# Branch D's value products in pairs of heads, with features on partitions

## The chip, the cores and the metric

The kernel runs on one core of a Trainium2 chip, in one launch. The metric is the device time of that core in microseconds (us), from the start to the end of the program. Three runs of the kernel before gave 691.07, 691.10 and 691.25 us, so the median is 691.1 us.

## What is computed

The model has two layers (DEPTH 2) over 512 positions of width 1024. In each layer the input is normalised and multiplied by one wide matrix `w_in`. Its columns feed four attention branches of four heads each: A (latent), B (dilated), C (sparse, top 128 keys of each query) and D (differential). Each branch's output is multiplied by SiLU of a gate, the four are put side by side and multiplied by `w_out`. Branch D is the one that changes:

```python
def diff_branch(q, k, v, lam_params, subln, table, lambda_init):
    ...
    p = jax.nn.softmax(s, axis=-1)
    a = p[:, 0] - lam * p[:, 1]
    return jnp.einsum('bhqs,bshd->bqhd', a.astype(v.dtype), v)
    ...
    o = rms_norm(o, subln) * (1.0 - lambda_init)
```

Each head has two softmax maps. They are combined with a learned weight, multiplied by the values (64 features a head), and every row of 64 features is normalised by its own root mean square and scaled by `subln`.

## The kernel before

There are no loops that the hardware runs: the Python writes out one long instruction stream for each engine. The order is the text `SCHEDULE` (line 109 on), a list of steps by hand. `sequence()` turns it into one list of (layer, step), and each engine's block walks the same list from the first step to the last and emits what that step wants of it. So an engine that stands at a wait of one step starts nothing of the later steps, and where a step stands in the text decides what lies ahead of it in each queue.

The steps that matter here:

- `unit X c`: 24 matmuls of TensorE (three products for each of 8 slices of the contraction) that give 128 columns of the projection for 512 tokens. ScalarE writes the rounded high part out of PSUM (line 815), VectorE writes the rest (line 1044). Units take turns in two PSUM banks.
- `CONVERT_AT` (from `convert_steps`): after some steps ScalarE turns the next weights into their high part (line 726, two instructions), and GpSimd makes the low part (line 684). The function puts a conversion where steps of a certain cost have passed since the buffer came free: a token unit costs 1, another unit 2, a `pv` 1.
- `scores j a b`: products of queries and keys of job j, blocks a to b-1, through three PSUM banks in turn. VectorE adds the bias (line 1085, "shifted"), which frees the bank, then ScalarE takes the exponential (line 834). Jobs 0 to 3 are branch D's heads, with 8 blocks each (two maps of 4), jobs 4 to 7 are B's.
- `norm j`: for D, VectorE combines the two maps (lines 989 to 994).
- `turn j kb`: TensorE transposes a block column of probabilities into one of two PSUM banks (line 1365), and ScalarE copies it to `turned[j % 2]` (line 847), which frees the bank. TensorE's `turn` waits until the copy of the turn two before it is done. The first copy of job j waits for the `pv` of job j - 2.
- `pv i`: the product with the values. TensorE waits until every `turn` of its jobs is copied. For D one head is one step with 10 small matmuls, queries on partitions (line 1386). For B, C and A a pair of heads is one step with 8 matmuls, features on partitions, the two heads in the two halves of the partitions (line 1393).
- For D, VectorE multiplies each head by the reciprocal of its sum into `od` (line 1104). `dsquares` squares and sums on VectorE (1116 to 1118), GpSimd takes the power -1/2 (line 691), `dscale` multiplies (1123), `dnorm` transposes on TensorE (1402) and multiplies into the gate (1130).
- For B, C and A, `wide i` spreads the reciprocals over 512 columns on ScalarE (line 857), `spread i` transposes them on TensorE (1411) and VectorE multiplies them into the gate (1095); VectorE then multiplies the product in (1111).
- `topk n`: n rounds of the selection for branch C, all on VectorE (lines 980 and 981).

Of the kernel before, what the change touches and what calls it, by code (L numbers as in the profile page):

```python
# [39 lines left out]
for _n, _w in (("cq", 192), ("ckv", 128), ("kr", 32), ("ga", 256), ("bq", 256), ("bk", 256), ("bv", 256),  # L40
# [45 lines left out]
NWIDE = NPV - HEADS  # L86
# [31 lines left out]
    scores 7 0 3, topk 1, topk 2, turn 5 2, fill 8, norm 6, turn 5 3, topk 1, unit gc 0, fill 9, topk 3, scores 7 3 4, unit gc 1, norm 7, turn 6 0, fill 10, spread 4, fill 11, pv 4, turn 6 1, turn 6 2  # L118
    scores 8 0 2, turn 6 3, turn 7 0, scores 8 2 4, wide 5, turn 7 1, unit ga 0, aload, turn 7 2, turn 7 3, spread 5, pv 5
    scores 9 0 1, turn 8 0, turn 8 1, norm 8, aup_head, unit ga 1, mix 6, turn 8 2, scores 9 1 4, aup 0, turn 8 3, aup 1, turn 9 0, norm 9  # L120
    scores 10 0 1, turn 9 1, aturn 0, wide 6, scores 10 1 4, aup 2
    scores 11 0 1, turn 9 2, scores 11 1 4, norm 10, spread 6, turn 9 3, aturn 1, pv 6, aup 3, turn 10 0, aturn 2, turn 10 1, turn 10 2, mix 7, norm 11, turn 10 3, aturn 3, turn 11 0, turn 11 1, wide 7
    scores 12 0 2, scores 12 2 4
    scores 13 0 2, spread 7, turn 11 2, turn 11 3, scores 13 2 4, norm 12, mix 3, pv 7, mix 2, turn 12 0, turn 12 1, turn 12 2, norm 13, turn 12 3, turn 13 0
    scores 14 0 2, turn 13 1, wide 8, turn 13 2, scores 14 2 4
    scores 15 0 1, norm 14, mix 4, mix 5, turn 13 3, scores 15 1 4, spread 8, norm 15, turn 14 0, pv 8, ya 0, wide 9, turn 14 1, turn 14 2, turn 14 3, turn 15 0, turn 15 1, spread 9, turn 15 2, turn 15 3, ya 2, pv 9, mix 0, mix 1, ya 1
# [39 lines left out]
def units_of(step):  # L166

    k = step[0]
    if k == "u":
        return ["dve", "dve"]  # L170
    if k == "unit":
        if step[1] in ("cv", "dv", "bv", "ckv"):
            return ["act"]
        return ["act"] if step[1:] == ("cq", 0) else ["dve"]
    if k in ("dnorm", "spread"):
# [44 lines left out]
ROOTS = [(l, s) for l, s in SEQUENCE if s[0] in ("hmean", "dsquares", "aup_head", "y")]  # L220
# [67 lines left out]
def trunk(nc, x, w_in, w_out, norm_pre, norm_post, mla_q_norm, mla_kv_norm, mla_w_uq, mla_w_ukv,  # L288
# [8 lines left out]
    with ExitStack() as ctx:  # L297
# [60 lines left out]
        odsq = at("odsq", "staging", [P, NB, 2, HD], F32)  # L358
# [3 lines left out]
        od = at("od", "staging", [P, NB, 2, HD], F32, skip=2 * KB)  # L362
# [40 lines left out]
        dsum = tiny("dsum", [P, 2 * NB])  # L403
# [53 lines left out]
        od_ready, a_folded, lat_squared = sem("od_ready"), sem("a_folded"), sem("lat_squared")  # L457
# [29 lines left out]
        def gate_of(i):  # L487

            br, h = JOBS[PV_JOBS[i][0]]
            return 2 * "ABC".index(br) + h // 2  # L490

        def wait_gated(eng, l, k):

            if k >= 6:
                eng.wait_ge(emptied_by["dve"], emptied(l * NU + UNIT_AT[("dnorm", k - 6)], "dve"))
# [220 lines left out]
        def _(act):  # L716
# [44 lines left out]
            for l, step in SEQUENCE:  # L761
# [15 lines left out]
                if kind == "unit":  # L777
# [8 lines left out]
                    if name in ("bv",):  # L786
                        act.wait_ge(pv_ready, l * NPV + HEADS)
# [48 lines left out]
                if kind == "turn":  # L836
# [5 lines left out]
                    if kb == 0 and j == 0 and l > 0:  # L842
# [5 lines left out]
                                         ACT.Copy).then_inc(turn_emptied, 1)  # L848
                if kind == "wide":
# [65 lines left out]
        def _(dve):  # L915
# [42 lines left out]

            after(nc.vector.memset(means[:], 1.0))
# [23 lines left out]
            def normalise(l, j):  # L983
# [3 lines left out]
                if MAPS[j] == 2:  # L987
# [3 lines left out]
                                                         ALU.mult, ALU.mult))  # L991
                    for q in range(NB):
# [8 lines left out]
            for l, step in SEQUENCE:  # L1001
# [88 lines left out]
                if kind == "spread":  # L1090
                    n = l * NU + UNIT_AT[step]
                    k = gate_of(step[1])
                    wait_unit_emptied(dve, l * NU + UNIT_AT[("unit", "g" + "abcd"[k // 2], k % 2)])
                    dve.wait_ge(unit_ready, n + 1)
                    nc.vector.tensor_tensor(gate[:, k, :], bank[:, unit_bank(n), :], gate[:, k, :], ALU.mult  # L1095
                                            ).then_inc(emptied_by["dve"], 1)
                if kind == "pv":
                    j = PV_JOBS[step[1]][0]
                    br, h = JOBS[j]
                    dve.wait_ge(pv_ready, l * NPV + step[1] + 1)  # L1100
                    if br == "D":
                        if h % 2 == 0 and (h > 0 or l > 0):
                            dve.wait_ge(unit_ready, (l if h else l - 1) * NU + UNIT_AT[("dnorm", 0 if h else 1)] + 1)
                        nc.vector.tensor_tensor(od[:, :, h % 2, :],
                                                bank[:, PV, 0:NB * HD].rearrange("p (t d) -> p t d", d=HD),
                                                inv[:, j % 4, 0, :].unsqueeze(2).to_broadcast([P, NB, HD]),
                                                ALU.mult).then_inc(pv_emptied, 1)
                    else:
                        k = gate_of(step[1])
# [3 lines left out]
                if kind == "dsquares":  # L1113
                    r = ROOT_AT[l, step]
                    dve.wait_ge(pv_emptied, l * NPV + 2 * step[1] + 2)
                    after(nc.vector.tensor_tensor(odsq[:], od[:], od[:], ALU.mult))
                    after(nc.vector.tensor_reduce(dsum[:].rearrange("p (t h) -> p t h", h=2), odsq[:], AX_X, ALU.add))
                    nc.vector.tensor_scalar(means[:, r % 2, :], dsum[:], 1.0 / HD, EPS, ALU.mult, ALU.add
                                            ).then_inc(means_ready, 1)
                if kind == "dscale":  # L1120
                    r = ROOT_AT[l, ("dsquares", step[1])]
                    dve.wait_ge(roots_ready, r + 1)
                    nc.vector.tensor_tensor(od[:], od[:],
                                            roots[:, r, :].rearrange("p (t h) -> p t h", h=2).unsqueeze(3)
                                            .to_broadcast([P, NB, 2, HD]), ALU.mult).then_inc(od_ready, 1)
                if kind == "dnorm":
                    n = l * NU + UNIT_AT[step]
                    k = 6 + step[1]
# [49 lines left out]
                if kind == "y":  # L1178
# [4 lines left out]
                    after(nc.vector.tensor_tensor(dsum[:, 0:1], ysq[:, tb, 0:1], ysq[:, tb, 1:2], ALU.add))  # L1183
                    nc.vector.tensor_scalar(means[:, r % 2, 0:1], dsum[:, 0:1], 1.0 / DM, EPS,
# [16 lines left out]
        def _(pe):  # L1201
# [61 lines left out]
            for l, step in SEQUENCE:  # L1263
# [104 lines left out]
                if kind == "pv":  # L1368
# [11 lines left out]
                    if br == "D":  # L1380
# [143 lines left out]
```

## Time and profile before

| | |
|---|---|
| median of 3 runs | 691.1 us |
| span of the profiled execution | 689.9 us |
| TensorE matmul busy | 665.3 us, 96% |
| VectorE busy | 394.1 us, 57% |
| ScalarE busy | 338.7 us, 49% |
| GpSimd busy | 241.9 us, 35% |

The span runs from the first to the last instruction; the 1.2 us between it and the median lie outside of it. The granted clock of TensorE is 0.999 of full speed on average. The two layers repeat each other: what layer 0 does at a time t in the stretch of branch D, layer 1 does at t + 333.8 us.

### The profile page before, as it was taken

How to read it: one execution, taken by the hardware profiler on the slowest of the kernel's cores; microseconds unless marked ns; L12 is line 12 of the kernel's file. 1: busy time of each engine (PE TensorE's matmuls, PEld its weight loads, DVE VectorE, ACT ScalarE, POOL GpSimd, SP SyncE). 2: the span in 40 equal slices, each digit the busy share in tenths (PEclk: the TensorE clock that was granted, in tenths of full speed). 3: DMA queues.
4: the chain of work that ended last, by engine and by line, in shares of the span. 5: the costliest groups of instructions: out<-in, count | busy, mean ns of one | idle time of the engine just before them, and what ended most of it. 6: DMA issues, size and time to landing. Idle time of an engine off the chain costs nothing. (4 is left out here: it accounts for less than half of the span.)

```text
span 689.9 us, 10538 instructions
## 1 busy us (share of the span) xinstructions
PE 665.3 (96%) x3852; PEld 538.4 (78%) x3852; DVE 394.1 (57%) x982; ACT 338.7 (49%) x804; POOL 241.9 (35%) x209
## 2 busy tenths in 40 slices
PE   6999999999999999999999999999999999999996
PEld 4988877788887665679998897878788777556995
DVE  4413599868669375540470257985968755555114
ACT  5523634666333647952353355456543553787120
POOL 1442541434242942002424534325422467020030
PEclk9999999999999999999999999999999999999999
DMA  8448877323222213012362697552322220120202
GB/s 252 138 169 223 240 216 254 124 78 109 76 77 77 78 61 123 1 43 82 124 183 76 214 273 207 146 152 77 110 77 76 77 78 23 58 104 1 92 31 92
DMA packets 68763, 80.97 MB, mean 117 GB/s; under 512 B 12853, under 2 KB 54453, under 8 KB 68713
## 3 DMA queue, kind: packets, MB, share of 16 engines
q1 hardware_dynamic: 68713, 80.31, 38.1%
q8 instruction: 31, 0.51, 0.3%
q14 instruction: 19, 0.16, 0.1%
HBM read 69.77 MB, written 13.94 MB: 121 GB/s over the span
## 5 line engine op out<-in xcount | busy, mean ns | idle before, releaser
L684 POOL TENSOR_TENSOR w_low<-w_raw,w_high 128x512 fp32r<-128x512 f32 (+2 forms) x156 | 199.8, 1313 | 364.2 <-ACT w_high L726 364.1
L1236 PE MATMUL bank<-uT,w_high 128*128 128x512 f32 x400 | 159.7, 399 | 0.0
L1238 PE MATMUL bank<-uT,w_low 128*128 128x512 f32 x400 | 157.8, 394 | 0.0
L1237 PE MATMUL bank<-uT,w_high 128*128 128x512 f32 x400 | 157.4, 393 | 0.0
L834 ACT ACTIVATE probs<-probs,negmax 128x128 f32<-128x128 f32 (+3 forms) x160 | 88.8, 557 | 51.6 <-DVE negmax L1085 50.4
L726 ACT ACTIVATE w_high<-w_raw 128x1024 fp32r<-128x1024 f32 (+2 forms) x78 | 76.4, 1031 | 28.5 <-DMA w_raw<-in_w_out 24.4
L1236 PEld LDWEIGHTS bank<-uT,w_high 128*128 128x128 f32 x400 | 75.2, 188 | 17.4 <-issue 1.4
L1238 PEld LDWEIGHTS bank<-uT,w_low 128*128 128x128 f32 x400 | 75.0, 188 | 17.7
L1237 PEld LDWEIGHTS bank<-uT,w_high 128*128 128x128 f32 x400 | 75.2, 188 | 16.2
L1236 PE MATMUL bank<-w_high,mix 128*128 128x256 f32 x256 | 72.1, 282 | 0.2 <-DVE gate L1095 0.2
L1237 PE MATMUL bank<-w_low,mix 128*128 128x256 f32 x256 | 71.6, 280 | 0.0
L1238 PE MATMUL bank<-w_high,mix 128*128 128x256 f32 x256 | 71.6, 280 | 0.0
L1236 PE MATMUL bank<-w_high,uT 128*128 128x256 f32 (+1 forms) x192 | 56.5, 294 | 1.1 <-DVE uT L955 0.7
L1365 PE MATMUL bank<-ident,probs 128*128 128x128 f32 x320 | 52.1, 280 | 4.6 <-ACT turned L847 3.5
L1237 PE MATMUL bank<-w_low,uT 128*128 128x256 f32 (+1 forms) x192 | 55.1, 287 | 0.0
L1238 PE MATMUL bank<-w_high,uT 128*128 128x256 f32 (+1 forms) x192 | 55.0, 287 | 0.0
L980 DVE MAX8 best<-select 128x8 f32<-128x512 f32 (+2 forms) x96 | 53.6, 558 | 2.1
L847 ACT ACTIVATE turned<-bank 128x512 f32<-128x512 f32 (+3 forms) x128 | 50.6, 428 | 6.9 <-PE bank L1365 4.4
L1365 PEld LDWEIGHTS bank<-ident,probs 128*128 128x128 f32 x320 | 37.1, 140 | 19.8 <-ACT turned L847 7.7
L1085 DVE CUSTOM_DVE_ANT_0 probs<-bank,strips 128x128 f32<-128x128 f32 (+1 forms) x104 | 45.0, 471 | 13.0 <-PE bank L1238 10.5
L981 DVE MATCH_REPLACE8 select<-best,select 128x512 f32<-128x512 f32 (+2 forms) x96 | 52.1, 543 | 0.0
L1236 PEld LDWEIGHTS bank<-w_high,mix 128*128 128x128 f32 x256 | 48.2, 188 | 0.9 <-issue 0.5
(153 smaller groups left out, 1048.1 us busy)
## 6 DMA issues: line engine op xcount, KB each, us to landing
w_raw<-in_w_in SPq DMA_DIRECT2D x27, 1024.0 KB, 5.5
w_raw<-in_w_out SPq DMA_DIRECT2D x8, 1024.0 KB, 4.9
parts_dram<-staging SPq DMA_DIRECT2D x12, 512.0 KB, 5.6
strips<-strips_dram SPq DMA_DIRECT2D x24, 256.0 KB, 5.6
dqk<-parts_dram SPq DMA_DIRECT2D x24, 256.0 KB, 4.4
hX<-in_x SPq DMA_DIRECT2D x8, 512.0 KB, 5.4
qidx<-parts_dram SPq DMA_DIRECT2D x12, 256.0 KB, 4.3
w_raw<-in_w_in SPq DMA_DIRECT2D x4, 512.0 KB, 5.6
```

Of the source, the lines that this page charges most:

```text
L684: ins = nc.gpsimd.tensor_tensor(w_low[:, s, ks, 0:w], w_raw[:, s, ks, 0:w], w_high[:, s, ks, 0:w].bitcast(F32), ALU.subtract)
L726: nc.scalar.activation(w_high[:, g % SLOTS, ks, 0:w], w_raw[:, g % SLOTS, ks, 0:w], ACT.Copy).then_inc(w_high_done, 1)
L834: nc.scalar.activation(pr, pr, ACT.Exp, bias=negmax[:, j % 4, m, q:q + 1], scale=-1.0, accum_out=sums[:, j % 4, m, q:q + 1]).then_inc(exp_ ...
L847: nc.scalar.activation(turned[j % 2][:, TOFF[kb]:TOFF[kb] + w], bank[:, TURN + t % 2, 0:w], ACT.Copy).then_inc(turn_emptied, 1)
L980: after(nc.vector.max(best[:], row))
L981: after(nc.vector.match_replace(row, best[:], row, MARK))
L1085: nc.vector.tensor_tensor_reduce(sl, bank[:, SCORE + n % 3, 0:WID[q]], bias, -1.0, 3.0e38, ALU.add, ALU.min, negmax[:, j % 4, m, q:q + 1]) ...
L1236: nc.tensor.matmul(out_ap, lh, rh, start=start, stop=False)
L1237: nc.tensor.matmul(out_ap, lh, rl, start=False, stop=False)
L1238: return nc.tensor.matmul(out_ap, ll, rh, start=False, stop=stop)
L1365: ins = nc.tensor.transpose(bank[:, TURN + t % 2, (q - kb) * P:(q - kb + 1) * P], buf[:, POFF[q] + kb * P:POFF[q] + (kb + 1) * P], ident[:])
```

## The change

Branch D's products go as the other branches' do: `PV_JOBS` holds pairs for all heads, so `pv 0` takes jobs 0 and 1, `pv 1` jobs 2 and 3, and the old `pv 4` to `pv 9` become `pv 2` to `pv 7`. The steps `dsquares`, `dscale` and `dnorm` go. In their place ScalarE squares the product out of PSUM into `dsq`, and the new step `dsum` multiplies `dsq` by a 128x2 matrix of ones and zeros (`pairs`), which gives the sums of squares of the two heads for each query. VectorE makes means of them, with an epsilon multiplied by the squared sum of the exponentials, so that the division by that sum drops out. GpSimd takes the roots as before, and `wide` and `spread` bring them into rows.

```diff
-PV_JOBS = [(j,) for j in range(HEADS)] + [(j, j + 1) for j in range(HEADS, NJ, 2)]
+PV_JOBS = [(j, j + 1) for j in range(0, NJ, 2)]
...
-    scores 2 0 2, norm 1, unit bq 0, scores 2 2 3, topk 1, unit bq 1, turn 1 0, turn 1 1, scores 2 3 6, pv 0, scores 2 6 8, norm 2, turn 1 2, turn 1 3, unit bk 0, turn 2 0, turn 2 1
-    scores 3 0 1, scores 3 1 4, turn 2 2, topk 4, unit bk 1, scores 3 4 6, pv 1, scores 3 6 8, turn 2 3, dsquares 0, norm 3, dscale 0, squares_a
-    scores 4 0 3, unit cqq 0, turn 3 0, dnorm 0, scores 4 3 4, topk 5, turn 3 1, pv 2, unit cqq 1, turn 3 2
-    scores 5 0 2, turn 3 3, topk 1, unit ck 0, turn 4 0, norm 4, turn 4 1, topk 1, scores 5 2 4, topk 1, turn 4 2, turn 4 3, topk 1, pv 3, topk 1, topk 1, topk 1, unit ck 1, topk 1
-    scores 6 0 1, unit bv 0, topk 1, unit bv 1, unit bv 2, norm 5, dsquares 1, scores 6 1 4, dscale 1, topk 1, turn 5 0, turn 5 1, asums, topk 1, topk 2, unit bv 3, topk 1, topk 1, topk 1, wide 4, dnorm 1
...
+    scores 2 0 2, norm 1, unit bq 0, scores 2 2 3, topk 1, unit bq 1, turn 1 0, turn 1 1, scores 2 3 6, turn 1 2, turn 1 3, scores 2 6 8, norm 2, pv 0, unit bk 0, turn 2 0, turn 2 1, dsum 0
+    scores 3 0 1, scores 3 1 4, turn 2 2, topk 4, unit bk 1, scores 3 4 6, scores 3 6 8, turn 2 3, wide 0, norm 3, squares_a
+    scores 4 0 3, unit cqq 0, turn 3 0, spread 0, scores 4 3 4, topk 5, turn 3 1, unit cqq 1, turn 3 2
+    scores 5 0 2, turn 3 3, topk 1, pv 1, unit ck 0, turn 4 0, norm 4, turn 4 1, topk 1, scores 5 2 4, topk 1, dsum 1, turn 4 2, turn 4 3, topk 1, topk 1, topk 1, wide 1, topk 1, unit ck 1, topk 1
+    scores 6 0 1, unit bv 0, topk 1, unit bv 1, unit bv 2, norm 5, spread 1, scores 6 1 4, topk 1, turn 5 0, turn 5 1, asums, topk 1, topk 2, unit bv 3, topk 1, topk 1, topk 1, wide 2
...
@@ scalar @@
+                if kind == "pv" and step[1] < NPD:
+                    i = step[1]
...
+                    act.wait_ge(pv_ready, l * NPV + i + 1)
+                    nc.scalar.activation(dsq[:], bank[:, PV, :], ACT.Square).then_inc(d_squared, 1)
...
+                    if i < NPD:
+                        r = ROOT_AT[l, ("dsum", i)]
+                        act.wait_ge(roots_ready, r + 1)
+                        nc.scalar.activation(wide[i % 2][:].rearrange("p q h d -> p (q h) d"),
+                                             roots[:, r, :].unsqueeze(2).to_broadcast([P, 2 * NB, HD]),
+                                             ACT.Copy).then_inc(wide_ready, 1)
@@ vector @@
+                    nc.vector.scalar_tensor_tensor(desq[:, j, :], sums[:, i, 0], EPS, sums[:, i, 0],
+                                                   ALU.mult, ALU.mult)
...
+                        dve.wait_ge(d_squared, l * NPD + step[1] + 1)
+                        nc.vector.scalar_tensor_tensor(gate[:, k, :], bank[:, PV, :], subln[:, l:l + 1],
+                                                       gate[:, k, :], ALU.mult, ALU.mult).then_inc(pv_emptied, 1)
...
+                if kind == "dsum":
...
+                    nc.vector.scalar_tensor_tensor(means[:, r % 2, :].rearrange("p (t h) -> p t h", h=2),
+                                                   bank[:, unit_bank(n), 0:2 * NB].rearrange("p (t h) -> p t h", h=2),
+                                                   1.0 / HD, desq[:, 2 * i:2 * i + 2, :].rearrange("p h t -> p t h"),
+                                                   ALU.mult, ALU.add).then_inc(means_ready, 1)
+                    nc.vector.tensor_copy(ysum[:], bank[:, unit_bank(n), 0:1]).then_inc(emptied_by["dve"], 1)
@@ tensor @@
-                    if br == "D":
-                        hs = slice(HD * h, HD * (h + 1))
-                        tr = turned[j % 2]
-                        for q in range(NB):
-                            for kb in range(q + 1):
-                                a = TOFF[kb] + (q - kb) * P
-                                ins = nc.tensor.matmul(bank[:, PV, HD * q:HD * (q + 1)], tr[:, a:a + P], v[:, kb, hs],
-                                                       start=kb == 0, stop=kb == q)
...
+                if kind == "dsum":
...
+                    pe.wait_ge(d_squared, l * NPD + step[1] + 1)
+                    b = work_bank(n)
+                    for q in range(NB):
+                        ins = nc.tensor.matmul(b[:, 2 * q:2 * q + 2], dsq[:, q * P:(q + 1) * P], pairs[:],
+                                               start=True, stop=True)
```

`pv` steps count in `convert_steps`. With the new schedule the weights `bv` (group 13) are converted at `unit cqq 1` and no longer at the old `pv 2`; the other conversions keep their places.

## Rows read from the trace of the kernel before

**Rows 1.** The page's busy times, by engine, with instructions.

```profile
PE 665.3 (96%) x3852; PEld 538.4 (78%) x3852; DVE 394.1 (57%) x982; ACT 338.7 (49%) x804; POOL 241.9 (35%) x209
```

**Rows 2.** Busy times by stretch: us, engines, clock, DMA share, GB/s; D's stretch of layer 0.

```profile
139.00:215.00 76.00, 75.49 (x445) 62.73 (x444) 57.14 (x165) 38.78 (x97) 27.04 (x21) 1.00 0.28 89
```

**Rows 3.** Timeline of TensorE around pv 0: start, length, line, idle before.

```profile
139.51 2.34 PE L1386 MATMUL bank<-values,turned 128*128 128x64 f32 x20
141.66 0.65 PE L1339 MATMUL bank<-dqk 96*128 96x384 f32 x2
142.15 0.49 PE L1365 MATMUL bank<-ident,probs 128*128 128x128 f32 x3
142.40 0.48 PE L1236 MATMUL bank<-uT,w_high 128*128 128x512 f32 x1
```

**Rows 4.** Timeline of TensorE, a pair of branch B and what follows it.

```profile
226.49 2.37 PE L1393 MATMUL bank<-turned,values 128*64 128x512 f32 x16
228.80 0.55 PE L1365 MATMUL bank<-ident,probs 128*128 128x128 f32 x3
229.56 0.44 PE L1365 MATMUL bank<-ident,probs 128*128 128x128 f32 x2 [0.22 <-ACT turned L847]
```

**Rows 5.** Timeline of ScalarE around pv 0.

```profile
139.03 2.00 ACT L726 ACTIVATE w_high<-w_raw 128x1024 fp32r<-128x1024 f32 x2
140.92 0.97 ACT L847 ACTIVATE turned<-bank 128x512 f32<-128x512 f32 x2
...
143.35 0.61 ACT L834 ACTIVATE probs<-probs,negmax 128x384 f32<-128x384 f32 x1
...
144.66 0.54 ACT L847 ACTIVATE turned<-bank 128x256 f32<-128x256 f32 x2
```

**Rows 6.** Timeline of TensorE around the old pv 1.

```profile
156.24 2.34 PE L1386 MATMUL bank<-values,turned 128*128 128x64 f32 x20
...
160.94 0.50 PE L1236 MATMUL bank<-uT,w_high 128*128 128x512 f32 x1
```

**Rows 7.** Timeline of VectorE around the old pv 1.

```profile
156.98 0.69 DVE L1044 SCALAR_TENSOR_TENSOR bqk<-bank,bqk 128x512 fp32r<-128x512 f32 x1 [0.82 <-ACT bqk L815]
157.58 0.28 DVE L1085 CUSTOM_DVE_ANT_0 probs<-bank,strips 128x128 f32<-128x128 f32 x1
...
159.47 0.69 DVE L1085 CUSTOM_DVE_ANT_0 probs<-bank,strips 128x512 f32<-128x512 f32 x1
```

**Rows 8.** Timeline of ScalarE around unit cqq 1 and turn 3 3.

```profile
176.92 0.60 ACT L815 ACTIVATE cqk<-bank 128x512 fp32r<-128x512 f32 x1 [3.52 <-PE bank L1238]
177.42 0.38 ACT L847 ACTIVATE turned<-bank 128x256 f32<-128x256 f32 x1
178.48 0.40 ACT L834 ACTIVATE probs<-probs,negmax 128x128 f32<-128x128 f32 x1 [0.69 <-DVE negmax L1085]
...
179.38 0.25 ACT L847 ACTIVATE turned<-bank 128x128 f32<-128x128 f32 x1
```

**Rows 9.** Timeline of TensorE there: turns 3 2 and 3 3, unit ck 0.

```profile
176.66 0.38 PE L1365 MATMUL bank<-ident,probs 128*128 128x128 f32 x2
...
177.86 0.33 PE L1365 MATMUL bank<-ident,probs 128*128 128x128 f32 x1
177.94 0.48 PE L1236 MATMUL bank<-uT,w_high 128*128 128x512 f32 x1
```

**Rows 10.** Timeline of VectorE at norm 0: the small instruction.

```profile
115.33 0.22 DVE L990 SCALAR_TENSOR_TENSOR coef<-inv,neglam,sums 128x4 f32<-128x4 f32 x1
```

**Rows 11.** Timeline of ScalarE in layer 1: its copies of turns 1 0 and 1 1.

```profile
474.70 0.97 ACT L847 ACTIVATE turned<-bank 128x512 f32<-128x512 f32 x2
```

**Rows 12.** Timeline of TensorE: the last matmul.

```profile
682.87 0.28 PE L1238 MATMUL bank<-w_high,mix 128*128 128x256 f32 x1
```

**Rows 13.** Busy times by stretch after the last matmul, columns as in rows 2.

```profile
685.00:687.00 2.00, 0.00 (x0) 0.00 (x0) 1.75 (x2) 0.00 (x0) 0.00 (x0) 1.00 0.00 0
687.00:689.00 2.00, 0.00 (x0) 0.00 (x0) 0.00 (x0) 0.00 (x0) 0.00 (x0) 0.81 0.64 262
```

More of the change, by code:

```diff
@@ new lines @@
+    scores 5 0 2, turn 3 3, topk 1, pv 1, unit ck 0, turn 4 0, norm 4, turn 4 1, topk 1, scores 5 2 4, topk 1, dsum 1, turn 4 2, turn 4 3, topk 1, topk 1, topk 1, wide 1, topk 1, unit ck 1, topk 1
+    scores 6 0 1, unit bv 0, topk 1, unit bv 1, unit bv 2, norm 5, spread 1, scores 6 1 4, topk 1, turn 5 0, turn 5 1, asums, topk 1, topk 2, unit bv 3, topk 1, topk 1, topk 1, wide 2
+    scores 7 0 3, topk 1, topk 2, turn 5 2, fill 8, norm 6, turn 5 3, topk 1, unit gc 0, fill 9, topk 3, scores 7 3 4, unit gc 1, norm 7, turn 6 0, fill 10, spread 2, fill 11, pv 2, turn 6 1, turn 6 2
@@ L120 @@
+    scores 8 0 2, turn 6 3, turn 7 0, scores 8 2 4, wide 3, turn 7 1, unit ga 0, aload, turn 7 2, turn 7 3, spread 3, pv 3
     scores 9 0 1, turn 8 0, turn 8 1, norm 8, aup_head, unit ga 1, mix 6, turn 8 2, scores 9 1 4, aup 0, turn 8 3, aup 1, turn 9 0, norm 9
-    scores 10 0 1, turn 9 1, aturn 0, wide 6, scores 10 1 4, aup 2
-    scores 11 0 1, turn 9 2, scores 11 1 4, norm 10, spread 6, turn 9 3, aturn 1, pv 6, aup 3, turn 10 0, aturn 2, turn 10 1, turn 10 2, mix 7, norm 11, turn 10 3, aturn 3, turn 11 0, turn 11 1, wide 7
+    scores 10 0 1, turn 9 1, aturn 0, wide 4, scores 10 1 4, aup 2
@@ L127 @@
+    scores 14 0 2, turn 13 1, wide 6, turn 13 2, scores 14 2 4
+    scores 15 0 1, norm 14, mix 4, mix 5, turn 13 3, scores 15 1 4, spread 6, norm 15, turn 14 0, pv 6, ya 0, wide 7, turn 14 1, turn 14 2, turn 14 3, turn 15 0, turn 15 1, spread 7, turn 15 2, turn 15 3, ya 2, pv 7, mix 0, mix 1, ya 1
 """
@@ L174, in units_of @@
         return ["act"] if step[1:] == ("cq", 0) else ["dve"]
-    if k in ("dnorm", "spread"):
+    if k in ("dsum", "spread"):
         return ["dve"]
@@ L216, in highs @@
     return full * UNIT_HIGH.count(True) + UNIT_HIGH[:rest].count(True)
-ROOTS = [(l, s) for l, s in SEQUENCE if s[0] in ("hmean", "dsquares", "aup_head", "y")]
+ROOTS = [(l, s) for l, s in SEQUENCE if s[0] in ("hmean", "dsum", "aup_head", "y")]
 ROOT_AT = {r: i for i, r in enumerate(ROOTS)}
@@ L402, in trunk @@
         ysq = tiny("ysq", [P, NB, 2])
-        dsum = tiny("dsum", [P, 2 * NB])
+        desq = tiny("desq", [P, HEADS, NB])
+        ysum = tiny("ysum", [P, 1])
+        pairs = tiny("pairs", [P, 2])
         means = tiny("means", [P, 2, 8])
@@ L489, in gate_of @@
             br, h = JOBS[PV_JOBS[i][0]]
[L490 removed]
+            return 2 * "ABCD".index(br) + h // 2
         def wait_gated(eng, l, k):
             if k >= 6:
[L495 removed]
+                wait_unit_emptied(eng, l * NU + UNIT_AT[("spread", k - 6)])
             else:
@@ L956, in low_u @@
                                             uT[:, 0, ks, ts].bitcast(F32), ALU.subtract).then_inc(emptied_by["dve"], 1)
+            for half in range(2):
+                for h in range(2):
+                    nc.vector.memset(pairs[HD * half:HD * (half + 1), h:h + 1], float(h == half))
             after(nc.vector.memset(means[:], 1.0))
@@ L1097, in _ @@
                 if kind == "pv":
-                    j = PV_JOBS[step[1]][0]
-                    br, h = JOBS[j]
-                    dve.wait_ge(pv_ready, l * NPV + step[1] + 1)
-                    if br == "D":
[L1102 to L1107, printed above, removed]
+                    k = gate_of(step[1])
+                    if step[1] < NPD:
+                        wait_unit_emptied(dve, l * NU + UNIT_AT[("unit", "gd", k % 2)])
+                        dve.wait_ge(d_squared, l * NPD + step[1] + 1)
+                        nc.vector.scalar_tensor_tensor(gate[:, k, :], bank[:, PV, :], subln[:, l:l + 1],
+                                                       gate[:, k, :], ALU.mult, ALU.mult).then_inc(pv_emptied, 1)
                     else:
-                        k = gate_of(step[1])
+                        dve.wait_ge(pv_ready, l * NPV + step[1] + 1)
                         wait_unit_emptied(dve, l * NU + UNIT_AT[("spread", step[1])])
@@ L1112, in _ @@
                                                        ALU.mult, ALU.mult).then_inc(pv_emptied, 1)
-                if kind == "dsquares":
+                if kind == "dsum":
+                    i = step[1]
+                    n = l * NU + UNIT_AT[step]
                     r = ROOT_AT[l, step]
[L1115 to L1128, printed above, removed]
-                    dve.wait_ge(unit_ready, n + 1)
-                    nc.vector.scalar_tensor_tensor(gate[:, k, :], bank[:, unit_bank(n), :], subln[:, l:l + 1],
-                                                   gate[:, k, :], ALU.mult, ALU.mult).then_inc(emptied_by["dve"], 1)
+                    dve.wait_ge(unit_ready, n + 1)
+                    nc.vector.scalar_tensor_tensor(means[:, r % 2, :].rearrange("p (t h) -> p t h", h=2),
[3 more added lines that the diff above has]
+                    nc.vector.tensor_copy(ysum[:], bank[:, unit_bank(n), 0:1]).then_inc(emptied_by["dve"], 1)
                 if kind == "aup_head":
@@ L1182, in _ @@
                     dve.wait_ge(roots_ready, r - 1)
-                    after(nc.vector.tensor_tensor(dsum[:, 0:1], ysq[:, tb, 0:1], ysq[:, tb, 1:2], ALU.add))
-                    nc.vector.tensor_scalar(means[:, r % 2, 0:1], dsum[:, 0:1], 1.0 / DM, EPS,
+                    after(nc.vector.tensor_tensor(ysum[:], ysq[:, tb, 0:1], ysq[:, tb, 1:2], ALU.add))
+                    nc.vector.tensor_scalar(means[:, r % 2, 0:1], ysum[:], 1.0 / DM, EPS,
                                             ALU.mult, ALU.add).then_inc(means_ready, 1)
```

59 lines of the change are left out of this document (27 added, 32 removed).

## The prediction

> **What bounds the kernel.** I read the busy times first. TensorE's matmuls fill 96% of the span and no other engine passes 57% [rows 1]. In the stretch of branch D they fill 75.5 of 76 us at full clock [rows 2]. So a matmul that goes saves its time, and a wait of TensorE that comes costs its time. VectorE and ScalarE count only where they hold TensorE up. That is read from the timelines, step by step in the order of the schedule: what each engine has in its queue ahead of what TensorE waits for. Layer 1 repeats layer 0: its copies of turns 1 0 and 1 1 begin at 474.70, those of layer 0 at 140.92 [rows 5, 11]. I walk through layer 0 and double the result.
>
> **The matmuls.** A single head of D holds TensorE from 139.51 to 141.66, 2.15 us for 20 passes of 128x64, or 0.107 each [rows 3]. A pair of another branch takes 226.49 to 228.80, 2.31 us for two heads [rows 4]. Per layer four singles (8.60) become two pairs (4.62), 3.98 less. Each `dsum` adds 4 matmuls with a stationary 128x128 block, in the same two passes as D's singles, so 8. No row shows two moving columns. I take the 0.107 of the passes of 64 columns, whose stationary block has the same size, so 0.86 a step and 1.72 a layer. The low end is half a pass price, 0.43; the high end is 8 passes that don't overlap at all, 2.2 (the 0.275 of one record's length). `spread 0` and `spread 1` are four transposes each in the place of the four of `dnorm`: nothing. Work alone is -2.26 us a layer.
>
> The page TensorEngine Tiling (Array Packing) of the Trainium skill, section Performance Considerations, speaks for the swap: with a moving side of 64 or less, swap the operands and tile the columns twice. The rows agree (2.31 for two heads against 4.30), so by that rule alone the change gains.
>
> **VectorE, ScalarE, GpSimd.** VectorE loses some 4 us a pair and gains about 2. ScalarE gains one square and one `wide`. None of this is on the path as busy time: VectorE is idle before most of these places. The roots have time: `dsum 0` is over before unit bk 1 (5.7 us), its root is wanted after it; `dsum 1` is followed by unit ck 1. One small thing is on the path: the instruction for `desq` stands ahead of the four that combine the maps of job 0, and `turn 0 0` waits for those. It costs as much as L990 at most, 0.22 [rows 10]; I take 0.15 a layer, with 0 to 0.25 as ends.
>
> **The waits, in the order of the schedule.** Here lies the price. `pv 0` and `pv 1` stood where TensorE would otherwise have waited; now they go elsewhere.
>
> Place 1, turns 1 2 and 1 3. TensorE has written turns 1 0 and 1 1 before 139.5, but ScalarE is converting weights until 141.0 and copies them from 140.92 to 141.89 [rows 5]. `turn 1 2` needs the first of the two banks. Before, `pv 0` lay between and nothing was lost: turns 1 2 and 1 3 went at 142.15 [rows 3]. Now `turn 1 2` is due at 139.51 and waits until about 141.55, `turn 1 3` until 141.95. Two score blocks follow to about 142.6 (they took 0.49 [rows 3]).
>
> Place 2, the pair `pv 0` waits for the copy of `turn 1 3`. ScalarE's queue has turns 1 0 and 1 1, three exponentials until 143.35 [rows 5], and then the two copies, which took 0.54 [rows 5]: 143.9. With 0.05 for the restart the pair runs from 143.95 to 146.26 and unit bk 0 starts at 146.26 where it started at 142.40 [rows 3]. Places 1 and 2: +3.86, of which 3.7 is waiting (2.0 and 1.35, and restarts). Behind the waiting TensorE stands everything.
>
> `dsum 0`: +0.86.
>
> Place 3, the score blocks of job 3 without the old `pv 1` between them. Block 7 needs the bank of block 4, which VectorE shifts from 157.58 to 157.86, behind the low part of unit bk 1 [rows 7]. TensorE would be ready at 156.5. With VectorE's four shifts close up, the last starts at 158.6 and not at 159.47 [rows 7], and all behind it (the blocks of job 4, then unit cqq 0 at 160.94 [rows 6]) moves by that: -0.87 where a single [rows 6] of 2.15 us went. So 1.28 becomes a wait.
>
> The old `pv 2` goes: -2.15. It stood ahead of cqq 1 with nothing waiting, so this one is a true gain.
>
> Place 4, the pair `pv 1` right behind `turn 3 3`. Call T the end of unit cqq 1 (176.66 [rows 9]). Before, ScalarE wrote cqq 1's high part to T+0.76, copied turn 3 2, waited for the shifts, took two exponentials and copied turn 3 3 at T+2.72 to T+2.97 [rows 8]; nobody hurried, since unit ck 0 started at T+1.28 [rows 9]. Now the pair needs that copy. And the conversion of `bv` (2.0 us, as in rows 5) falls to cqq 1 and lies in front: high part to T+0.76, conversion to T+2.7, turn 3 2 to T+3.0, exponentials (0.90 [rows 8]) to T+3.9, copy to T+4.13. The pair starts at T+4.18, ends at T+6.49, and ck 0 starts 5.21 later than before, 2.9 of it waiting.
>
> `dsum 1` +0.86, the old `pv 3` -2.15. Behind it nothing waits: VectorE's rounds of `topk` decide the low part of ck 1, some 1.5 us behind TensorE, and the next use of that bank comes over 3 us after it.
>
> **The sum.** Per layer 3.86 + 0.86 - 0.87 - 2.15 + 5.21 + 0.86 - 2.15 + 0.15 = +5.8 us; that is -2.1 of work and +7.9 of waits. Twice is +11.5. The profiled execution had a span of 689.9, so 701.4, and the median lies 1.2 above the span: 702.6. Downstream I find nothing to take it back: in the rest of a layer TensorE waits only briefly, and for copies that move with it.
>
> **Rivals.** *Work alone decides*, if ScalarE's queue is not as full as I read it: 2 x (-2.1) = -4.2, 686.9, faster. For it: TensorE is the bound. Against it: the copies at 140.92 are in the trace behind the conversion, and a turn of TensorE is seen to wait for such a copy even behind a pair (0.22 [rows 4]). A chance of 0.11, since two of the four waits would have to go before the sign turns (from 5.8 saved a layer on).
>
> *The conversion at cqq 1 does not stand in the way* (it moves, or I have its place wrong). Then `pv 1` starts at T+3.0 at the latest row, some 1.1 earlier, with shifts that come sooner up to 1.9: -2.3 to -3.8, 698.8 to 700.3. A chance of 0.12.
>
> *The clock falls in the new waits.* Price: matmuls at 1.2 in place of 2.4 GHz take double; if that lasted as long as one unit of 5.7 us in each layer, +5.7 each, 714. Against it: the last matmul ends at 683.15 [rows 12] and the granted clock is still 1.00 until 687, falling only then [rows 13]; that is 3.8 us idle, and my longest wait is 2.9. A chance of 0.04. The page TensorE: Matmul & The Clock Gate of the Trainium skill, Part 1, says that an idle TensorE is throttled to half rate and that gaps in the middle of a kernel cost this way; the trace agrees for its tail only.
>
> *A part of the waits is absorbed later* so that the time ends within 0.2% (1.4 us, about what a measurement of this kernel can tell from no change): 0.03. The forecast itself has 0.70.
>
> **The range.** The unknown of `dsum` gives -1.7 to +5.4 in all, `desq` -0.3 to +0.2, and restarts after four waits a layer, at 0.05 to 0.2 each, up to +1.2. They don't add up at their ends. With the second rival that is 698 to 707. Slower by over 0.2%: 0.86, within: 0.03, faster: 0.11.
>
> **What would show it.** In the profile after, TensorE's turn line (L1365's successor) should wait about 2 us for the copy in front of turn 1 2, once a layer; the line of the pairs should wait 1.3 and 2.9 us for copies in front of `pv 0` and `pv 1`; ScalarE should run the conversion right behind the high part of cqq 1; the eight passes of `dsum` should take 0.9 us; TensorE's busy time should fall by about 4 us while the span grows. I am wrong if the pairs of D start without a wait, if `dsum` takes over 2 us a step, or if the granted clock drops inside the span.

## The result and the profile after

The changed kernel takes 712.5 us (median of four runs, 706.3 to 719.6) against 691.1 before. The ratio is 1.029, with a 95% interval of 1.024 to 1.034. It is slower, as forecast, but by 21 us and not by 11.5, outside of the range. Its runs differ by 13 us among themselves, those of the kernel before by 2, and the slower a run the lower its mean granted clock of TensorE: 0.988 at 706.3, 0.983 at 711.7, 0.979 at 713.4 and 0.969 at 719.6, the run that was profiled. The kernel before has 0.995 to 0.999 in the runs beside the experiments. The run of 719.6 us counts as a slow one and is left out of the ratio; the other three have a median of 711.7.

The lines below are of that slowest run, so they show the loss at its largest; the profile of experiment e3, at 713.7 us, has low stretches of the clock at the same three places of each layer, three of the six half as long.

The page of the kernel after, first the busy times (to set beside rows 1), then TensorE's granted clock in 40 slices, in tenths:

```profile
PE 678.7 (95%) x3788; PEld 536.8 (75%) x3788; DVE 385.5 (54%) x982; ACT 343.0 (48%) x812; POOL 239.8 (33%) x209
...
PEclk9999999988899999999999999998889999999999
```

There are 64 matmul records fewer and yet TensorE is busy for 13 us more. The clock row (PEclk, 9 stands for 90% or more) says why: in three slices of each layer it ran below full speed. Those are the slices of branch D.

Who TensorE waited for in branch D's stretch of layer 0 (columns: us in total, times, longest). In the kernel before there was one wait here, of 0.5 us; the lines of before, L1365, L1393 and L1339, are L1376, L1395 and L1350 now:

```profile
PE bank L1395 <- ACT turned L848: 3.4, 2, 2.6
PE bank L1376 <- ACT turned L848: 1.9, 1, 1.9
PE bank L1350 <- DVE negmax L1105: 1.5, 2, 1.3
```

TensorE's timeline around turns 1 2 and 1 3 and the pair `pv 0`, which answers to rows 3 and, for the form of the pair, to rows 4 (start, length, what, idle before):

```profile
138.33 0.71 PE L1350 MATMUL bank<-dqk 96*128 96x512 f32 x3
140.94 0.83 PE L1376 MATMUL bank<-ident,probs 128*128 128x128 f32 x3 [1.90 <-ACT turned L848]
141.42 1.09 PE L1350 MATMUL bank<-dqk 96*128 96x384 f32 x2
143.32 4.54 PE L1395 MATMUL bank<-turned,values 128*64 128x512 f32 x16 [0.81 <-ACT turned L848]
147.78 0.69 PE L1247 MATMUL bank<-uT,w_high 128*128 128x512 f32 x1
```

Both waits are where the prediction put them; the second is 0.81 us and not 1.35, since the score blocks ahead of it took longer. But the pair takes from 143.32 to 147.78, 4.46 us, where the same form took 2.31 in rows 4. ScalarE in the same stretch, to set beside rows 5:

```profile
138.40 1.99 ACT L727 ACTIVATE w_high<-w_raw 128x1024 fp32r<-128x1024 f32 x2
140.29 0.97 ACT L848 ACTIVATE turned<-bank 128x512 f32<-128x512 f32 x2
...
142.72 0.54 ACT L848 ACTIVATE turned<-bank 128x256 f32<-128x256 f32 x2
```

Busy times by stretch (columns as in rows 2; the number before the last two is the granted clock), first from turns 1 2 on, then around place 3, then around place 4:

```profile
139.00:141.00 2.00, 0.10 (x2) 0.07 (x2) 1.47 (x7) 2.00 (x4) 1.48 (x2) 1.00 0.97 261
141.00:148.00 7.00, 6.19 (x22) 2.65 (x23) 3.62 (x11) 3.66 (x14) 3.49 (x3) 0.53 0.34 111
148.00:150.00 2.00, 2.00 (x9) 1.64 (x10) 0.75 (x1) 0.50 (x1) 0.00 (x0) 0.95 0.00 0
...
165.00:172.00 7.00, 7.00 (x20) 5.42 (x20) 5.25 (x15) 5.16 (x17) 4.08 (x4) 0.52 0.64 215
...
186.00:193.00 7.00, 6.19 (x21) 3.18 (x22) 0.99 (x2) 1.35 (x6) 3.52 (x3) 0.53 0.36 125
```

A clock of 0.52 in a stretch of 7 us is 1.2 GHz in nearly all of it, the lower of the two levels. The first two begin when TensorE is at work again, at 141.4 and 165.3 us, 2.3 and 2.5 us after it had stopped. The third begins at 185.8, 1.5 us after it had stopped and 1 us before it starts again. Each lasts 6.8 us, and layer 1 has the same three. Over 61 us of each layer the mean is 0.83, so 2 x 0.17 x 61 = 21 us a layer ran at half rate. The other terms stand in the timelines as forecast: `dsum 0` takes 0.82 us,

```profile
154.43 0.95 PE L1404 MATMUL bank<-pairs,dsq 128*128 128x2 f32 x8
155.25 0.65 PE L1350 MATMUL bank<-dqk 96*128 96x128 f32 x3
```

and in front of `pv 1` ScalarE works through exactly the queue that was read from rows 8 and 9, with the conversion of the `bv` weights in it:

```profile
182.96 0.60 ACT L816 ACTIVATE cqk<-bank 128x512 fp32r<-128x512 f32 x1 [4.03 <-PE bank L1249]
183.46 2.00 ACT L727 ACTIVATE w_high<-w_raw 128x1024 fp32r<-128x1024 f32 x2
185.35 0.38 ACT L848 ACTIVATE turned<-bank 128x256 f32<-128x256 f32 x1
...
186.49 0.27 ACT L848 ACTIVATE turned<-bank 128x128 f32<-128x128 f32 x1
```

### The profile page after: what moved, and what is told of

It reads as the page before. It is cut to its first block and busy times, and to the rows that moved or that the text cites. A ratio compares the mean times of both kernels' runs of the same rounds, so it can differ in the third digit from the quotient of the medians.

```text
span 717.8 us, 10430 instructions
## 1 busy us (share of the span) xinstructions
PE 678.7 (95%) x3788; PEld 536.8 (75%) x3788; DVE 385.5 (54%) x982; ACT 343.0 (48%) x812; POOL 239.8 (33%) x209
## 5 line engine op out<-in xcount | busy, mean ns | idle before, releaser
L685 POOL TENSOR_TENSOR w_low<-w_raw,w_high 128x512 fp32r<-128x512 f32 (+2 forms) x156 | 197.5, 1298 | 344.7 <-ACT w_high L727 344.6
L1247 PE MATMUL bank<-uT,w_high 128*128 128x512 f32 x400 | 162.9, 407 | 0.0
L1249 PE MATMUL bank<-uT,w_low 128*128 128x512 f32 x400 | 159.9, 400 | 0.0
L1248 PE MATMUL bank<-uT,w_high 128*128 128x512 f32 x400 | 159.7, 399 | 0.0
L1247 PEld LDWEIGHTS bank<-uT,w_high 128*128 128x128 f32 x400 | 77.1, 193 | 19.6 <-issue 3.1
L1249 PEld LDWEIGHTS bank<-uT,w_low 128*128 128x128 f32 x400 | 76.5, 191 | 18.2
L1248 PEld LDWEIGHTS bank<-uT,w_high 128*128 128x128 f32 x400 | 77.0, 193 | 16.6
L1376 PE MATMUL bank<-ident,probs 128*128 128x128 f32 x320 | 52.6, 281 | 8.0 <-ACT turned L848 7.3
L692 POOL TENSOR_TENSOR roots<-means,minus_half 128x1 f32<-128x1 f32 (+1 forms) x22 | 18.7, 850 | 111.5 <-DVE means L1138 49.2
L1376 PEld LDWEIGHTS bank<-ident,probs 128*128 128x128 f32 x320 | 37.2, 141 | 23.1 <-ACT turned L848 12.3
L1395 PE MATMUL bank<-turned,values 128*64 128x512 f32 (+3 forms) x256 | 46.6, 516 | 7.7 <-ACT turned L848 7.7
```

What stands on the lines that cost most here:

```text
L685: ins = nc.gpsimd.tensor_tensor(w_low[:, s, ks, 0:w], w_raw[:, s, ks, 0:w], w_high[:, s, ks, 0:w].bitcast(F32), ALU.subtract)
L692: nc.gpsimd.tensor_tensor(roots[:, r, 0:n], means[:, r % 2, 0:n], minus_half[:, 0:n], ALU.pow).then_inc(roots_ready, 1)
L1247: nc.tensor.matmul(out_ap, lh, rh, start=start, stop=False)
L1248: nc.tensor.matmul(out_ap, lh, rl, start=False, stop=False)
L1249: return nc.tensor.matmul(out_ap, ll, rh, start=False, stop=stop)
L1376: ins = nc.tensor.transpose(bank[:, TURN + t % 2, (q - kb) * P:(q - kb + 1) * P], buf[:, POFF[q] + kb * P:POFF[q] + (kb + 1) * P], ident[:])
```

## The experiments

The theory to test had two halves: the loss comes from waits that the new order makes and not from the new arithmetic; and behind the waits TensorE's clock falls, which costs as much again. The rivals: the new matmuls themselves are dear, or throttle the clock; or the time goes elsewhere.

**e1: the waits filled.** The same kernel, and TensorE works on throwaway products while it waits.

```diff
+            def keep_busy(l, done, n):
+                pe.wait_ge(pv_emptied, l * NPV + done)
+                for _ in range(n):
+                    nc.tensor.matmul(bank[:, PV, 0:P], ident[:], ident[:], start=True, stop=True)
...
+                        if (j, i) == (3, 7):
+                            keep_busy(l, 1, 5)
...
+                if step == ("turn", 1, 2):
+                    keep_busy(l, 0, 9)
...
+                if kind == "pv" and step[1] < NPD:
+                    keep_busy(l, step[1], (5, 12)[step[1]])
```

> The changed kernel with throwaway 128x128 matmuls of TensorE into the idle bank of the products, at the four places where it waits: 9 before turn 1 2, 5 before pv 0, 5 before the last score block of job 3, 12 before pv 1 (0.21 us each, a little less than each wait). Theory: the loss is the waits for ScalarE's and VectorE's queues plus what the fallen clock adds, and the clock falls only because TensorE idles. Then the granted clock is back at 0.995 or more and the time is the one forecast without a fall, 699 to 703, 6 to 13 below the changed kernel. Rival: the clock falls because of the form of the new matmuls, or the time is lost elsewhere: then it stays at 706 or more, or rises by the added 13 us of matmuls.

Measured: 702.5 us (702.0 to 703.1), ratio to before 1.017 (1.015 to 1.019), clock 0.996 in every run. A kernel with some 13 us more of matmuls (62 of them, at the 0.21 us that I had counted for each) is 10 us faster. In this order the rival is out: the pairs and `dsum` are all in it, and they neither cost more than forecast nor pull the clock down. Its trace has no low stretch before TensorE's last matmul. TensorE's timeline, with the throwaway matmuls (L1271, on the line of the helper) in the waits:

```profile
138.04 0.71 PE L1358 MATMUL bank<-dqk 96*128 96x512 f32 x3
138.60 2.17 PE L1271 MATMUL bank<-ident 128*128 128x128 f32 x18
140.65 0.71 PE L1386 MATMUL bank<-ident,probs 128*128 128x128 f32 x3
141.11 0.66 PE L1358 MATMUL bank<-dqk 96*128 96x384 f32 x2
141.61 1.28 PE L1271 MATMUL bank<-ident 128*128 128x128 f32 x10
143.04 2.37 PE L1407 MATMUL bank<-turned,values 128*64 128x512 f32 x16
```

The pair is back at its old length, and its stretch at full clock:

```profile
139.00:200.00 61.00, 60.45 (x334) 47.72 (x334) 40.09 (x119) 30.22 (x78) 18.30 (x14) 1.00 0.25 75
```

This run is also the check of the forecast's sum, since it has its waits and not the fallen clock: 702.5 against 702.6.

**e6 and e7: one wait, without the pairs.** e6 is the kernel before with one thing of the change, the order of turns 1 2 and 1 3; e7 fills that wait as e1 does.

```diff
-... scores 2 3 6, pv 0, scores 2 6 8, norm 2, turn 1 2, turn 1 3, unit bk 0 ...
+... scores 2 3 6, turn 1 2, turn 1 3, scores 2 6 8, norm 2, pv 0, unit bk 0 ...
```

> The kernel before, unpaired, with only one thing of the change: turns 1 2 and 1 3 go ahead of pv 0, which follows norm 2. TensorE then waits about 2.0 us a layer for ScalarE's copy behind its conversion. Theory: the wait alone costs 4 us in all, 695, if the clock holds, and up to 3 us more a layer, 701, if this one wait is enough for it to fall. Rival (the waits only appear with pairs): 691, as before.

> The kernel before with turns 1 2 and 1 3 ahead of pv 0 (as in e6, 703), and 9 throwaway matmuls (1.9 us) in that wait. Theory: the wait itself costs 2.0 us a layer and the rest of e6's 12 us is the clock: 695 with the clock at 0.997. Rival (the order costs in another way): stays near 703.

Measured: e6 703.1 us (699.2 to 704.2), ratio 1.017 (1.013 to 1.020). e7 695.6 (693.7 to 696.2), ratio 1.005 (1.0035 to 1.0065). So two transposes and a product that change places cost 12 us in a kernel of 691: some 4 for the waiting, as read from rows 5, and some 8 for the clock. That was more than the upper end that I gave for e6. Its profiled run has a low stretch of 6.8 us behind the wait in layer 0 and one of 10.2 us in layer 1. The busy times of e6 after the wait:

```profile
143.00:150.00 7.00, 7.00 (x27) 6.18 (x27) 3.46 (x11) 2.15 (x8) 2.08 (x2) 0.51 0.18 41
```

**e2: pv 1 behind unit ck 0.** One step moved, so that 5.7 us of matmuls lie between `turn 3 3` and the pair.

```diff
-    scores 5 0 2, turn 3 3, topk 1, pv 1, unit ck 0, turn 4 0, ...
+    scores 5 0 2, turn 3 3, topk 1, unit ck 0, pv 1, turn 4 0, ...
```

> The changed kernel with one step moved: pv 1 stands behind unit ck 0 and not behind turn 3 3. Theory: the wait in front of pv 1 (2.6 us a layer) goes and with it the low clock that follows it (about 6.8 us at half rate, some 3 us a layer): 9 to 12 below the changed kernel, near 701, and no low clock between 180 and 200 us of the span. Rival (the waits are not what costs): within 2 us of the changed kernel.

Measured: 706.7 us (702.0 to 708.3), ratio to before 1.022 (1.018 to 1.026), 5 to 6 us below the changed kernel; the wait of 2.6 us in front of `pv 1` is gone. The 5.2 us of waiting came back and hardly more: I expected 9 to 12. The other half of what I expected did come in the profiled run, the one of 702.0 us: between 180 and 200 us its clock is 1.00. It has low stretches of 6.8 and 3.4 us in layer 0 and one of 3.4 in layer 1, where the wait of 1.3 us at place 3 has none behind it. Runs of this kernel still have clocks of 0.978 to 0.987. Four runs each don't tell how often the third stretch was low in the changed kernel.

**e3: the conversion of bv back at its old place.**

```diff
+        if g == 13:
+            s = ("turn", 3, 1)
         at.setdefault(s, []).append(g)
```

> The changed kernel with only the conversion of the bv weights put back to its old place, behind turn 3 1 and ahead of unit cqq 1. Theory: ScalarE's copy of turn 3 3 then comes 1.1 to 1.4 us earlier, the wait in front of pv 1 falls from 2.6 to 1.2 to 1.5, and if that is too short for the clock to fall, 3 us more a layer come back: 3 to 9 below the changed kernel. The other two low stretches of each layer stay. Rival (the conversion isn't in the way): within 1 us of the changed kernel, wait 2.6.

Measured: 712.3 us (709.8 to 714.0), ratio to before 1.030 (1.027 to 1.032), no different from the changed kernel. The copy did come earlier, and the wait fell from 2.6 to 1.75, less than expected: TensorE now waits for the exponentials and the copy.

```profile
184.85 0.49 ACT L837 ACTIVATE probs<-probs,negmax 128x256 f32<-128x256 f32 x1
185.25 0.19 ACT L837 ACTIVATION_READ_ACCUMULATOR probs<-probs,negmax 128x1 f32 x1
185.34 0.25 ACT L850 ACTIVATE turned<-bank 128x128 f32<-128x128 f32 x1
```

Twice 0.85 us saved is within the scatter that the clock makes, and the clock still falls in this wait. So the conversion does stand in the way, against the second rival of the prediction, but it is 0.85 us of the wait and a small part of the time.

**e4 and e5: the pairs in an order without waits.** The arithmetic of the change is kept; only the schedule is new (and in e5 the place of one conversion). e5:

```diff
-    ... unit bq 0, scores 2 2 3, topk 1, unit bq 1, turn 1 0, turn 1 1, scores 2 3 6, turn 1 2, turn 1 3, scores 2 6 8, norm 2, pv 0, unit bk 0, turn 2 0, turn 2 1, dsum 0
-    scores 3 0 1, scores 3 1 4, turn 2 2, topk 4, unit bk 1, scores 3 4 6, scores 3 6 8, turn 2 3, wide 0, norm 3, squares_a
-    scores 5 0 2, turn 3 3, topk 1, pv 1, unit ck 0, turn 4 0, ...
+    ... unit bq 0, scores 2 2 5, topk 1, unit bq 1, turn 1 0, turn 1 1, scores 2 5 8, turn 1 2, turn 1 3, norm 2, unit bk 0
+    scores 3 0 1, scores 3 1 3, pv 0, scores 3 3 4, turn 2 0, turn 2 1, topk 4, unit bk 1, scores 3 4 6, turn 2 2, dsum 0, turn 2 3, scores 3 6 8, norm 3, squares_a, wide 0
+    scores 5 0 2, turn 3 3, topk 1, unit ck 0, pv 1, turn 4 0, ...
+        if g == 11:
+            s = ("norm", 2)
         at.setdefault(s, []).append(g)
```

e4 had turns 1 2 and 1 3 behind `unit bk 0`, `pv 0` behind `scores 3 1 4`, and the conversion where it was.

> The changed kernel with the steps around both pairs of branch D in another order: five score blocks of job 2 ahead of unit bq 1, turns 1 2 and 1 3 behind unit bk 0, pv 0 behind the first four score blocks of job 3, dsum 0 between the last two blocks of job 3, pv 1 behind unit ck 0. Theory: the pairing itself saves 2.1 us of matmuls a layer, and all the rest was the order: 686 to 689, faster than the kernel before, clock 0.997 or more. Rival (a pair costs more than its matmuls show, or dsum does): 692 or more.

> The changed kernel in a second new order. The first one (e4) left one wait: TensorE stood 2.1 us before the fourth score block of job 3, since VectorE's norm 2 came late (it waited for exponentials that stand behind ScalarE's conversion of the cqq weights) and the low part of unit bk 0 stands behind it. Now that conversion stands behind norm 2, turns 1 2 and 1 3 go ahead of unit bk 0, and pv 0 lies between the third and the fourth score block of job 3. Theory: what e4 lost against the 687 it should have reached was this wait (2 x 2.1) and the low clock after it; without both the pairing shows its 2.1 us a layer: 686 to 689, faster than before by 2 to 5 us, clock 0.997 or more. Rival (something else in the pairs costs): 692 or more, as e4.

Measured: e4 697.1 us (693.2 to 700.8), ratio 1.009 (1.006 to 1.012). That is not the 686 to 689 of the theory but in the rival's range, 692 or more. Its trace has one large wait left, once in each layer:

```profile
148.25 0.50 PE L1350 MATMUL bank<-dqk 96*128 96x512 f32 x1 [2.10 <-DVE negmax L1105]
```

VectorE's `norm 2` waited for exponentials behind ScalarE's conversion, and the low part of `unit bk 0` stood behind `norm 2`. But the clock did not fall behind this wait, in either layer. It fell 13 us later, where TensorE waits for no more than 0.17 us (here 161 to 165; layer 1 has the same):

```profile
149.00:157.00 8.00, 8.00 (x46) 5.89 (x43) 5.59 (x17) 3.09 (x9) 0.00 (x0) 1.00 0.01 2
157.00:161.00 4.00, 3.83 (x25) 2.92 (x24) 2.90 (x12) 3.34 (x8) 1.72 (x2) 1.00 0.58 148
161.00:165.00 4.00, 4.00 (x11) 2.94 (x12) 2.14 (x5) 3.32 (x10) 4.00 (x4) 0.57 0.93 297
```

From 157.4 to 161.4 TensorE does small work there: score blocks of job 3, three transposes, the passes of `dsum 0`, and short products with `bqk`. So a wait is one way to a fall and not the only one. e5 moves that conversion and puts `pv 0` there. It takes 688.0 us (684.7 to 692.6, twelve runs) against 691.3 of the kernel before beside it, ratio 0.9953 (0.9933 to 0.9974): 0.5% faster than the kernel before, and 3.4% faster than the changed one. So e4's rival, that a pair or `dsum` costs more than its matmuls show, is out. Its TensorE waits 0.17 us at the last score block of job 3, which cost 1.33 in the changed kernel, and the pair stands between score blocks:

```profile
144.60 0.58 PE L1352 MATMUL bank<-dqk 96*128 96x128 f32 x3
145.10 2.38 PE L1397 MATMUL bank<-turned,values 128*64 128x512 f32 x16
147.41 0.51 PE L1352 MATMUL bank<-dqk 96*128 96x512 f32 x1
...
155.99 0.49 PE L1352 MATMUL bank<-dqk 96*128 96x512 f32 x1 [0.17 <-DVE negmax L1107]
```

Its profiled run, the one of 686.0 us, has no low stretch before TensorE's last matmul. The kernel before was not run in this new order, but the traces tell what is order and what is arithmetic: TensorE's idle time is the same, 24.6 us before (689.9 less 665.3) and 24.7 in e5 (684.2 less 659.5), and its busy time fell to 659.5 us from 665.3 [rows 1]:

```profile
PE 659.5 (96%) x3788; PEld 526.2 (77%) x3788; DVE 386.7 (57%) x982; ACT 343.2 (50%) x812; POOL 241.6 (35%) x209
```

**e9, e8 and e10: one wait put back into e5.** e9 has `pv 1` directly behind `turn 3 3` again. e8 and e10 have the last score blocks of job 3 bare again; they differ in where `dsum 0` goes.

```diff
e8
-    ... turn 2 0, turn 2 1, topk 4, unit bk 1, scores 3 4 6, turn 2 2, dsum 0, turn 2 3, scores 3 6 8, norm 3, ...
+    ... turn 2 0, turn 2 1, dsum 0, turn 2 2, topk 4, unit bk 1, scores 3 4 6, scores 3 6 8, turn 2 3, norm 3, ...
e10
-    ... unit bk 1, scores 3 4 6, turn 2 2, dsum 0, turn 2 3, scores 3 6 8, norm 3, ...
+    ... unit bk 1, scores 3 4 6, scores 3 6 8, turn 2 2, turn 2 3, dsum 0, norm 3, ...
```

> e5 with place 4 as the change has it: pv 1 directly behind turn 3 3. Theory: the wait of 2.6 us a layer comes back, 5.2 in all, 693.2, and the clock falls after it, 3 us a layer more: 699. Rival (the wait only adds up with the ones before it): less than 693.

> e5 (the reordered pairs, 688.0) with place 3 as the change has it: dsum 0 goes back behind turn 2 1, so the last score blocks of job 3 follow each other with nothing between. Theory: TensorE waits 1.3 us a layer more at the last block (0.2 before): 2.2 us in all, 690.3. If a wait of this size is enough for the clock to fall after it, up to 3 us a layer more: 696. Rival (this place costs nothing by itself): 688.

> e5 with the last four score blocks of job 3 behind each other and turns 2 2, 2 3 and dsum 0 behind them, so that place 3 is bare and no second wait arises (e8 had one of 1.7 us at turn 2 2). Theory: 1.1 us a layer of waiting more than e5, 2.2 in all, 690.2 with the clock up; if the clock falls after this wait of 1.3 us alone, 3 us a layer more, 693 to 696. Rival (a wait of this size is free, and e8's 10.7 us were all from its other wait): 688.

Measured: e9 698.1 us (695.1 to 703.9), ratio 1.012 (1.005 to 1.018), near the 699 with a fall. Its profiled run shows the wait of 2.59 us in both layers and the fall in one of them. First the stretch with and behind the wait in layer 0, then in layer 1 (the wait ends at 176.2 and 511.6):

```profile
174.00:178.00 4.00, 1.77 (x10) 0.77 (x12) 1.63 (x7) 2.18 (x7) 4.00 (x4) 1.00 0.96 315
178.00:182.00 4.00, 4.00 (x23) 3.14 (x20) 0.75 (x1) 0.60 (x1) 0.96 (x1) 1.00 0.00 0
...
508.00:512.00 4.00, 1.41 (x9) 0.89 (x10) 2.96 (x10) 3.55 (x9) 2.62 (x3) 1.00 0.81 234
512.00:516.00 4.00, 4.00 (x18) 1.99 (x15) 0.00 (x0) 0.57 (x1) 2.33 (x2) 0.57 0.26 94
```

But that fall is only one of three of 3.4 us in this trace. The other two stand where those of e4 do, behind a wait of 0.17 us at the end of job 3's score blocks, in both layers (the first of them):

```profile
154.80 0.49 PE L1352 MATMUL bank<-dqk 96*128 96x512 f32 x1 [0.17 <-DVE negmax L1107]
...
157.00:161.00 4.00, 4.00 (x11) 3.13 (x11) 2.66 (x6) 2.80 (x7) 4.00 (x4) 0.57 0.86 257
```

So the distance from e5 to e9 is not the price of the one wait alone. e5 has this stretch too, and the lower clocks of its slower runs (0.988 at 692.6 us) may come from it; none of those was profiled.

e8 took 698.8 us (697.5 to 701.9), ratio 1.013 (1.009 to 1.017), above what I expected, but it was not the clean experiment that I meant: `dsum 0` and `turn 2 2` in their new place made a second wait of 1.7 us. e10 has none: 693.3 us (690.6 to 694.8), ratio 1.004 (1.002 to 1.006), 5 above e5, of which 2.3 are the wait itself. In its profiled run the clock fell behind the wait of 1.34 us in layer 0 (0.65 over 9 us) and not in layer 1. The fall begins at 157.7, in the passes of `dsum 0`, near where it came in e4 and e9 without such a wait, so it can't be put down to the wait alone:

```profile
156.41 0.50 PE L1352 MATMUL bank<-dqk 96*128 96x512 f32 x1 [1.34 <-DVE negmax L1107]
...
155.00:164.00 9.00, 7.66 (x30) 6.39 (x30) 7.29 (x24) 7.42 (x20) 6.58 (x5) 0.65 0.69 208
489.00:498.00 9.00, 7.66 (x43) 6.30 (x42) 7.25 (x21) 6.65 (x16) 6.64 (x5) 1.00 0.68 208
```

## Why the prediction was right and wrong

**The sign and its cause: right.** The work saved by the pairs is real (e5: 3.3 us faster in all, 5.8 less of TensorE's busy time, against 4.2 forecast for work alone), and the order that came with them took more than it gave.

**The waits: right, in place and in size.** Places 1 and 2: in e1 `unit bk 0` starts 7.23 us after ScalarE's conversion does (145.34 against 138.11), in the prediction 7.23 (146.26 against 139.03). Place 3: 1.33 us in the trace after, 1.28 forecast. Place 4: in the trace after, the pair starts 4.11 us behind the end of `unit cqq 1` (186.81 against 182.70), forecast 4.18. `dsum` took 0.82 and 0.91 us against 0.86, `desq` 0.16 against 0.15. The sum of all this was 702.6, and the kernel that has all of it and no fallen clock takes 702.5.

**The clock: wrong, and this is the step that failed.** The sum had no term for a fallen clock. The third rival, the clock that falls in the new waits, was given a chance of 0.04; it is what happened, on top of the forecast, and it is the 10 us between the changed kernel and e1. It was set aside by rows 12 and 13: TensorE stood for 3.8 us at the end of the span with the clock still at 1.00, and my longest wait was 2.9. That was one instance, and I took it for a bound. The same idle tail stands in all twelve traces, and in them the clock falls between 2.0 and 5.2 us after the last matmul: 5.1 in the kernel before, 2.5 in e1, whose last matmul ends at 692.5:

```profile
690.00:695.00 5.00, 2.51 (x22) 2.30 (x20) 2.10 (x5) 0.69 (x2) 0.55 (x1) 1.00 0.26 105
695.00:700.00 5.00, 0.00 (x0) 0.00 (x0) 1.20 (x1) 0.00 (x0) 0.00 (x0) 0.50 0.27 107
```

The row that I read was one of the latest by chance.

In the trace after, TensorE stopped at 139.0, took up work at 140.94, and the clock was low from 141.4 on: some 2.3 us after it had stopped, when it was already working again. In e9 2.59 us were followed by a fall in one layer and not in the other, in e10 1.34 us likewise, in e4 2.10 us in neither, and in e4 and e9 the clock fell in both layers behind 0.17 us. A wait of 1.3 to 2.6 us makes a fall possible, and here likely; whether it comes differs from layer to layer and from run to run. That is also why the runs of the changed kernel are spread over 13 us: what lies between their mean clocks of 0.988 and 0.969 is worth 13.8 us.

The page TensorE: Matmul & The Clock Gate of the Trainium skill, Part 1, section "A second HAM failure mode: psum-queue depth-cycling", tells of another kernel in which short idle gaps between groups of matmuls are frequent enough that the clock swings between its two levels. This trace agrees (0.53 over the 7 us from 141 on, and 1.00 again by 150).

**The price of a fall** had been set at 5.7 us a layer, for one unit at half rate. Each low stretch of the changed kernel's trace lasts 6.8 us and costs up to half of that, and there are three in a layer. Six of them are worth 20.5 us if TensorE had work all the time. Between this run and e1 the span differs by 17.6 us (717.8 and 700.2). The rest fell into time in which TensorE waited anyway, 0.8 to 1.1 us of each stretch of places 2 and 4. The three faster runs fit too, by their mean clocks: set against e1's, these say 5.7, 9.3 and 12.1 us, and the runs are 3.8, 9.1 and 10.9 us above e1's 702.5.

**The range.** Its upper end of 707 left this rival out by its chance. With three low stretches a layer, each behind a wait of 1.3 to 2.6 us, it should have reached 720.

Left open is what decides in a given layer whether a wait is followed by a fall, and why the clock falls in e4 and e9 in a stretch with hardly a wait. In both, `dsum 0` lies in that stretch; whether it has a part in this was not tested. No run here was made to find either.

## What to carry to other kernels

In a kernel that TensorE bounds, a wait of 1.3 us or more can cost more than its length: in e6 and e7 a wait of 2 us a layer cost 4 us as waiting and 8 as clock. One place in one trace where the clock held through an idle time is no proof that it holds through a shorter one. When steps move in an order by hand, ask of every step that leaves a place what it had been covering there, and read the other engines' queues at that place, the weight conversions above all. A way to separate the two costs is to fill the wait with throwaway matmuls: if the time falls, the clock was the loss, and the new arithmetic can be kept under another order.

## What the runs showed of the hardware that I had not expected

Added matmuls can make a kernel faster: e1 has 62 throwaway matmuls more than the changed kernel and takes 10 us less, since the granted clock stays at 0.996. And the mean granted clock of a run tells roughly how slow it is even where no trace was kept: the twelve runs of e5 go from 684.7 us at 0.998 to 692.6 us at 0.988, though six of them have 0.996 and lie between 686.0 and 689.3. A wait is not needed for a fall: in e4 and e9 the clock went to half rate for 3.4 us in both layers, with no wait longer than 0.17 us in the 8 us before.
